# Feed-forward blocks that project the gained residual, with the root factor applied on eviction, and first pieces made across the layer's end

## What is computed

```python
def rmsnorm(x, g):
    xf = x.astype(F32)
    y = xf * lax.rsqrt(jnp.mean(xf * xf, axis=-1, keepdims=True) + NORM_EPS)
    return (y * g.astype(F32)).astype(x.dtype)

def swiglu_ffn(h, w_gate, w_up, w_down):
    return (jax.nn.silu(h @ w_gate) * (h @ w_up)) @ w_down

    for l in range(DEPTH):
        h = rmsnorm(x, P['ffn1_norm'][l])
        x = x + 0.5 * swiglu_ffn(h, P['ffn1_w_gate'][l], P['ffn1_w_up'][l], P['ffn1_w_down'][l])
        h = rmsnorm(x, P['mix_norm'][l])
...
        x = x + jnp.concatenate([y_a, y_b, y_c], axis=-1) @ P['w_out'][l]
        h = rmsnorm(x, P['xattn_norm'][l])
...
        x = x + cross_attend(h, mk, mv, P['xattn_w_q'][l], P['xattn_w_o'][l])
        h = rmsnorm(x, P['ffn2_norm'][l])
        x = x + 0.5 * swiglu_ffn(h, P['ffn2_w_gate'][l], P['ffn2_w_up'][l], P['ffn2_w_down'][l])
    y = rmsnorm(x, P['final_norm'])
```

## Time and profile before

| | |
|---|---|
| median of 3 runs | 1805.14 us (1805.0 to 1806.65) |
| the profiled execution | 1805.17 us |
| its span | 1803.4 us |
| PE busy, share of the span | 1638.5 us, 91% |
| DVE, ACT, POOL busy | 57%, 40%, 19% |
| mean granted PE clock | 0.939 of full |

### The profile page before, as it was taken

One profiled execution on the slowest core, in us unless ns is written; L12 is line 12 of the kernel. 1 busy time (PEld: TensorE's weight loads), 2 busy tenths in 40 slices (PEclk: granted clock), 3 DMA queues, 4 the chain that ended last, 5 costly groups with the idle time before them and its releaser, 6 DMA issues.

```text
span 1803.4 us, 31820 instructions
## 1 busy us (share of the span) xinstructions
PE 1638.5 (91%) x13650; PEld 1536.5 (85%) x13650; DVE 1021.6 (57%) x1469; ACT 712.4 (40%) x1212; POOL 342.0 (19%) x365
## 2 busy tenths in 40 slices
PE   7999989897789988999989999998877998799997
PEld 6999979774679768999989998897646896799996
DVE  5555459958453336554365544698584642555543
ACT  5443345322444334443344433452234442444432
POOL 0000019993010010000000000399910000100000
PEclk9999989896899989999989999898869999899998
DMA  6666634104255763444345576340043558444440
GB/s 229 260 243 250 265 122 141 66 2 107 106 187 209 278 269 131 164 164 164 140 163 205 215 280 234 113 140 30 2 142 117 188 206 337 182 162 166 164 164 27
DMA packets 39244, 303.63 MB, mean 168 GB/s; under 512 B 4736, under 2 KB 4896, under 8 KB 6304
## 3 DMA queue, kind: packets, MB, share of 16 engines
q1 hardware_dynamic: 36624, 287.67, 43.6%
q0 software_dynamic: 2192, 12.35, 2.5%
q10 hardware_dynamic: 288, 1.57, 0.2%
HBM read 291.82 MB, written 36.83 MB: 182 GB/s over the span
## 4 chain that ended last, share of the span: by engine, by line
PE 66%; POOL 17%; DVE 9%; ACT 4%; DMA 3%; issue 1%; SPq 0%; POOLq 0%; DVEq 0%; ACTq 0%
PE bank L578 20%; PE bank L579 20%; PE bank L580 20%; POOL arena L474 12%; POOL arena L490 5%; DMA slots<-stream 3%; DVE w_lo L1610 2%; ACT w_hi L1218 2%; DVE h_mem L1625 1%; DVE rs L1620 1%; DVE h_lo L1610 1%; PE bank L589 1%; PE bank L1134 1%; PE bank L1170 1%; PE bank L1119 1%
## 5 line engine op out<-in xcount | busy, mean ns | idle before, releaser
L1610 DVE TENSOR_TENSOR w_lo<-slots,w_hi 128x1024 fp32r<-128x1024 f32 x392 | 481.9, 1232 | 430.1 <-ACT w_hi L1218 429.4
L578 PE MATMUL bank<-h_hi,w_hi 128*128 128x288 f32 x2048 | 620.1, 303 | 45.8 <-DVE h_lo L1610 30.2
L579 PE MATMUL bank<-h_lo,w_hi 128*128 128x288 f32 x2048 | 611.5, 299 | 0.0
L580 PE MATMUL bank<-h_hi,w_lo 128*128 128x288 f32 x2048 | 609.0, 297 | 0.0
L1218 ACT CAST w_hi<-slots 128x1024 fp32r<-128x1024 f32 x392 | 410.1, 1048 | 388.6 <-PE bank L580 346.6
L578 PEld LDWEIGHTS bank<-h_hi,w_hi 128*128 128x128 f32 x2048 | 389.8, 190 | 56.4 <-DVE h_lo L1610 37.4
L580 PEld LDWEIGHTS bank<-h_hi,w_lo 128*128 128x128 f32 x2048 | 392.8, 192 | 0.0
L579 PEld LDWEIGHTS bank<-h_lo,w_hi 128*128 128x128 f32 x2048 | 391.9, 191 | 0.2
L474 POOL TENSOR_SCALAR arena<-arena,par_all 128x256 f32<-128x256 f32 x240 | 210.4, 899 | 5.5
L579 PE MATMUL bank<-hid_lo,w_hi 128*128 128x288 f32 x704 | 208.2, 296 | 0.0
L578 PE MATMUL bank<-hid_hi,w_hi 128*128 128x288 f32 x704 | 208.1, 296 | 0.0
(11 more groups left out here) (279 smaller groups left out, 1934.9 us busy)
## 6 DMA issues: line engine op xcount, KB each, us to landing
slots<-stream SPq DMA_DIRECT2D x244, 1024.0 KB, 5.0
out_win3k<-win3k SPq DMA_DIRECT2D x2, 4080.0 KB
out_win3v<-win3v SPq DMA_DIRECT2D x2, 4080.0 KB
out_win2k<-win2k SPq DMA_DIRECT2D x2, 2032.0 KB
out_win2v<-win2v SPq DMA_DIRECT2D x2, 2032.0 KB
con<-consts SPq DMA_DIRECT2D x1, 2276.0 KB, 10.8
arena<-mem_in POOLq DMA_DIRECT2D x2, 1024.0 KB, 5.2
out_memk<-arena POOLq DMA_DIRECT2D x2, 1024.0 KB, 7.4
```

What stands on the lines that cost most here:

```text
L578: mm(out, lhs[0], rhs[0], start=start, stop=False)
L579: mm(out, lhs[0], rhs[1], start=False, stop=False)
L580: return mm(out, lhs[1], rhs[0], start=False, stop=stop)
L1610: D(tt(out, src, hi.bitcast(F32), ALU.subtract), name)
```

## The change

1. **Feed-forward blocks** no longer normalise. ACT makes `h_hi` as x times the norm's weight in one activation with a per-partition scale (`gained_hi`), DVE makes `h_lo` as x times the weight minus `h_hi` (`gained_lo`), and PE projects that. The factor `rs` (one over the root, per token) comes in afterwards: the gate's eviction is now two DVE products (`gs` is gate times rs, `gs2` is gs times rs), tanh reads `gs`, and gate times up takes `gs2` and the raw up bank.
2. **PE** runs `sum_squares` after the first gate unit instead of before it. Tile 0 uses banks 4 and 5, tile 1 banks 6 and 3.
3. **In front of ffn2** the gained pieces are made piece by piece inside the output projection: `gained_hi` then the square after each `x_o` on ACT, `gained_lo` of the piece before between the split and the addition on DVE.
4. **Across the layer's end** `next_layer` makes pieces 0 to 3 of the next layer's `h_hi`, `h_lo` and squares, and its first two weight units, before the second half of the down projection ends. POOL adds the four squares (`presum(l, "next", EARLY)`). Buffers of units run on across layers (`w_slot`). A prologue does the same before layer 0.
5. **Additions into x** after the down projection are signalled one by one, `("ffn2", "x", k)`, not per half.
6. In the last layer `next_layer` makes the four squares for the final norm, with tiny writes to `idle` in the place of the weight units.

The core of the diff (`KT` is 8). The constants and PE:

```diff
+EARLY = KT // 2
+PRESUM = {"ffn1": EARLY, "mix": EARLY, "xattn": KT - 1, "ffn2": KT - 1}
+        def ffn_banks(t):
+            return ((4, 5), (6, 3))[t] if t < 2 else ((t % 2) * 2, (t % 2) * 2 + 1)
...
                 def ffn(tag):
-                    sum_squares(tag)
                     for t in range(FT):
-                        gb, ub = (t % 2) * 2, (t % 2) * 2 + 1
+                        gb, ub = ffn_banks(t)
                         claim(gb, (VL, (tag, "gated", t)))
                         claim(ub, (VL, (tag, "hid", t)))
...
+                            if t == 0 and o == 0:
+                                sum_squares(tag)
...
-                                claim(b, (VL, (tag, "x", half)))
+                                claim(b, (VL, (tag, "x", 4 * half + d)))
```

On ACT, the two new functions:

```diff
+            def gained_hi(l, tag, k, name):
+                g = PAR[tag] + k
+                SL.done(fn(h_hi[:, k, :], x[:, k, :], ACT.Copy, scale=par_all[:, l, g:g + 1]), (name, "hi", k))
+            def next_layer(l):
+                at = min(l + 1, DEPTH - 1)
+                for k in range(EARLY):
+                    if l >= 0:
+                        act.wait_ge(vector_done, VL.value(l, ("ffn2", "x", k)))
+                    gained_hi(at, "ffn1", k, "next")
+                    SL.done(fn(sq[:, k, :], x[:, k, :], ACT.Square), ("next", "sq", k))
+                for u in range(EARLY_UNITS):
...
+                    copy(w_hi[:, w_slot(l + 1, u), :], raw_unit(u), ("next", "hi_w", u))
```

On ACT, between the cross attention and ffn2:

```diff
-                def ready2(k):
+                for k in range(KT):
                     if k:
                         split(next_unit(UNITS["o"] + k - 1))
                     act.wait_ge(vector_done, VL.value(l, ("x_o", k)))
...
+                    gained_hi(l, "ffn2", k, "ffn2")
+                    square("ffn2", x, T, k)
```

On DVE, in a tile of the feed-forward block:

```diff
+                        dve.wait_ge(tensor_done, TL.value(l, (tag, "gate", t)))
+                        D(tt(gs[:, t % 2, :], bank[gb][:, 0:T], rs[:], ALU.mult), (tag, "gated", t))
+                        settle()
+                        D(tt(gs2, gs[:, t % 2, :], rs[:], ALU.mult))
+                        if t > 1:
+                            split(next_unit(first + 2 * t))
+                        settle()
                         dve.wait_ge(scalar_done, SL.value(l, (tag, "tanh", t)))
-                        D(stt(th2[:, t % 2, :], th[:, t % 2, :], 1.0, bank[(t % 2) * 2][:, 0:T], ALU.add, ALU.mult),
+                        D(stt(th2[:, t % 2, :], th[:, t % 2, :], 1.0, gs2, ALU.add, ALU.mult))
```

On DVE, in the output projection of the cross attention:

```diff
                     if t:
                         split(next_unit(UNITS["o"] + t - 1))
+                        gained_lo(l, "ffn2", t - 1, "ffn2", l)
                     dve.wait_ge(tensor_done, TL.value(l, ("o", "cols", t)))
                     b = (5, 6, 7, 0, 1, 2, 3)[t % 7]
                     D(tt(x[:, t, :], bank[b][:, 0:T], x[:, t, :], ALU.add), ("x_o", t))
```

More of the change, by code:

```diff
@@ L190, in done @@
             self.last = ins
-        if name is not None:
+        if name is not None and self.recording:
             assert self.at.setdefault(name, self.n) == self.n, name
@@ L279, in program @@
         th2 = take(2, T)
+        gs = take(2, T)
+        gs2 = take(T)
         top[0] = KT * T
@@ L441, in store, with presum @@
                 stores[name] = n_stores[0]
-            pool.sem_inc(pool_done, PL.total)
+            def presum(l, tag, n):
+                for k in range(1, n):
+                    pool.wait_ge(scalar_done, SL.value(l, (tag, "sq", k)))
+                    if k > 1:
+                        pool.wait_ge(pool_done, PL.value(l, (tag, "added", k - 1)))
+                    PL.done(nc.gpsimd.tensor_tensor(sq[:, 0, :], sq[:, 0, :], sq[:, k, :], ALU.add), (tag, "added", k))
+            pool.sem_inc(pool_done, PL.tail)
+            PL.begin_prologue()
+            presum(-1, "next", EARLY)
             pool.wait_ge(con_landed, 32)
@@ L513, in _ @@
                 store(memv_out[l], vx, "memv")
-                presum("ffn2")
+                presum(l, "ffn2", PRESUM["ffn2"])
+                PL.begin_tail()
+                presum(l, "next", EARLY)
             assert n_stores[0] == NSTORE
@@ L532, in next_unit, with w_slot, next_or_own @@
             return u + NW if all(not u < end <= u + NW for end in RUN_ENDS) else None
+        def w_slot(l, u):
+            return (l * NUNIT + u) % NW
+        def next_or_own(l, tag, k):
+            return (l - 1, "next") if tag == "ffn1" and k < EARLY else (l, tag)
+        def ffn_banks(t):
+            return ((4, 5), (6, 3))[t] if t < 2 else ((t % 2) * 2, (t % 2) * 2 + 1)
         def unit_head(u):
@@ L1202, in _ @@
             l = DEPTH - 1
-            for k in range(KT):
-                pe.wait_ge(scalar_done, SL.value(l, ("final", "sq", k)))
+            pe.wait_ge(pool_done, PL.value(l, ("next", "added", EARLY - 1)))
+            for k in (0, *range(EARLY, KT)):
+                if k:
+                    pe.wait_ge(scalar_done, SL.value(l, ("final", "sq", k)))
                 i = mm(bank[7][:, 0:T], ones, sq[:, k, :], start=k == 0, stop=k == KT - 1)
@@ L1593, in _, with gained_lo, next_layer @@
             cp = nc.vector.tensor_copy
+            def gained_lo(l, tag, k, name, by):
+                g = PAR[tag] + k
+                dve.wait_ge(scalar_done, SL.value(by, (name, "hi", k)))
+                VL.done(stt(h_lo[:, k, :], x[:, k, :], par_all[:, l, g:g + 1], h_hi[:, k, :].bitcast(F32), ALU.mult, ALU.subtract),
+                        (name, "h_lo", k))
+            def next_layer(l):
+                at = min(l + 1, DEPTH - 1)
+                for k in range(EARLY):
+                    gained_lo(at, "ffn1", k, "next", l)
+                for u in range(EARLY_UNITS):
+                    if l == DEPTH - 1:
+                        VL.done(nc.vector.memset(idle[:, 2 + u:3 + u], 0.0), ("next", "lo", u))
+                        continue
+                    dve.wait_ge(scalar_done, SL.value(l, ("next", "hi_w", u)))
+                    w = w_slot(l + 1, u)
+                    VL.done(tt(w_lo[:, w, :], raw_unit(u), w_hi[:, w, :].bitcast(F32), ALU.subtract), ("next", "lo", u))
+            VL.begin_prologue()
+            next_layer(-1)
+            for k in range(EARLY, KT):
+                VL.done(nc.vector.memset(idle[:, k:k + 1], 0.0))
             for l in range(DEPTH):
@@ L1647, in ffn @@
                             split(next_unit(u))
-                        dve.wait_ge(tensor_done, TL.value(l, (tag, "down", half)))
+                        if half and tag == "ffn2":
+                            VL.begin_tail()
+                            next_layer(l)
                         for d in range(4):
                             k = 4 * half + d
+                            if d == 0:
+                                dve.wait_ge(tensor_done, TL.value(l, (tag, "down", half)))
                             D(stt(x[:, k, :], bank[4 + d if half == 0 else d][:, 0:T], 0.25, x[:, k, :], ALU.mult, ALU.add),
-                              (tag, "x", half) if d == 3 else None)
-                for u in range(NW):
-                    split(u)
+                              (tag, "x", k))
+                for k in range(EARLY, KT):
+                    gained_lo(l, "ffn1", k, "ffn1", l)
+                split(EARLY_UNITS)
                 ffn("ffn1")
@@ L2065, in _ @@
                     D(tt(x[:, t, :], bank[b][:, 0:T], x[:, t, :], ALU.add), ("x_o", t))
+                gained_lo(l, "ffn2", KT - 1, "ffn2", l)
                 split(next_unit(UNITS["o"] + KT - 1))
```

129 lines of the change are left out of this document (79 added, 50 removed).

## The result

The changed kernel takes 1782.31 us (median of four runs, 1780.0 to 1788.71) beside 1805.16 us before; the ratio is 0.988 with a 95% interval of 0.9865 to 0.9893. Run again later beside the kernel before, it took 1784.6 us against 1805.8, ratio 0.989 (0.9873 to 0.9907). The eight runs together have a median of 1784.0 us and a spread of 9.4 us. The kernel before stays within 1.65 us in the first series, but spreads by up to 8.9 us in the series of the experiments (1803.88 to 1812.77), so a difference of 2 or 3 us between two medians says little by itself. The predicted time was 1782.0, the range 1774 to 1791. The profiled execution took 1783.72 us, 21.45 less than that of before.

What follows compares the result with a forecast made beforehand. PE, busy 91% of the span, was taken as the bound, its idle time as the gain; 3.0 + 1.6 + 1.1 + 12.5 + 2.9 + 1.1 + 1.05 = 23.2 us off 1805.17 gave 1782.0 us, range 1774 to 1791.

Steps and rivals of the forecast that it cites:

- start: Kernel start, before layer 0: 3.0 us won; bounds 1.5 (slow clock throughout) and 4.5 (full clock).
- norm after ffn1: Norm behind the first feed-forward block: root 1.6 us earlier in layer 0, 2.9 in layer 1, 1.1 there at 1.2 GHz.
- ffn2's start: From output projection into second feed-forward block: 1.1 us won per layer; bounds 0.6 lost to 2.5 won, 7.5 with loop free.
- layer's end: From down projection into next layer's second weight unit: 12.5 us won, with a 0.6 us stall for piece 4, then full clock.
- last norm: Final norm: root 3.4 us after the first addition instead of 4.45, a gain of 1.05 us.
- attention stages: Stages between the feed-forward blocks: they move as a block, their waits for DMA stay, no gain.
- the loop doesn't bind: Rival at ffn2's start: PE's wait is one addition long, 6.4 us more won per layer, 1769; chance 0.11 (1765 to 1773).
- claim and loop: At ffn2's start: PE claims bank 5 before its first gate matmul; the DVE and ACT turn in `o` grows to 3.94 us.
- The table load: ACT's load takes 1.28 us, root right behind it, against the skill's 2.66; at the kernel's start it begins at 6.8.
- The tiles: 88 feed-forward tiles: two more DVE operations of 0.45 us each cost zero, with 0.4 us of cover per tile.
- the slower rival: DVE can't hold the feed-forward tile: at 0.35 us over, 88 tiles cost 30.8 us, 1813; chance 0.04.
- Restarts paid twice: Rival in the feed-forward blocks: units follow too late after the reciprocal, each block gives back 3 us, 1794; chance 0.10.

Runs made afterwards that it cites:

- The experiment that opens the loop: Changed kernel, but in `o` DVE adds each tile before making the next weight unit's rest and the previous tile's `h_lo`: 1770.73 us.
- both edits: Changed kernel with tile 0 on banks 4 and 6, tile 1 on 5 and 3, and DVE's addition in `o` ahead of rest and piece: 1767.57 us.

## Why the prediction was right, step by step

The total was right, and most of its steps too, but that it met the first median within 0.3 us is luck. The eight runs have 1784.0, and in the two profiles the steps add up to 1.7 and 2.9 us less than the forecast. The table sets them beside the two profiled executions of the kernel after (us won against the profiled execution of before).

| step | predicted | first | second |
|---|---|---|---|
| start | 3.0 | 2.05 | 3.01 |
| norm after ffn1, layer 0 (to the root) | 1.6 | 1.56 | 0.09 |
| ffn2's start, layer 0 | 1.1 | 1.16 | 1.29 |
| layer's end | 12.5 | 12.78 | 12.79 |
| norm after ffn1, layer 1 | 2.9 | 1.42 | 1.50 |
| ffn2's start, layer 1 | 1.1 | 1.40 | 1.35 |
| last norm | 1.05 | 1.0 | 1.0 |
| attention stages, both layers | 0 | +0.96 | +0.17 |
| four blocks, unit 1 to first addition | 0 | -0.85 | -0.85 |
| sum | 23.2 | 21.5 | 20.3 |

- **ffn2's start.** Size and mechanism were right: additions every 3.90 us (I said 3.94), a wait of 5.13, the second unit gained 1.16 us. Two small misses cancel in it: the clock stayed at 0.50 for 5.2 us, not 4.2, so the unit took 5.6 us and not 5.1, while PE started 0.3 us earlier than forecast and the two products took 0.75 us and not 1.0. I had refused the 7.5 us that one would expect at first sight. The experiment that opens the loop gives 7.4 and 7.2 us in the two layers. My rival "the loop doesn't bind" priced this at 6.4. Of the two reasons that I named, claim and loop, the loop is the stronger one, 13.3 us against 5.9.
- **The layer's end.** 12.78 against 12.5. The stall is 0.47, not 0.6, and full clock after it was the right choice. With the early pieces late this stage gives back 9.1 us, the largest single part of what the change wins. The 16.5 us by which that kernel is slower overstate it, since 5.9 of them are the edit's own cost at the last norm.
- **The norm after ffn1** is the mis-sized term. "At 3.4 after it the gain is 2.9" took full clock for PE's four products, and the root did come 3.44 us after the first addition in layer 0 of the first profile. Where the clock is slow it is 4.9, as in layer 1 of that profile and in both layers of the second. I had the low bound of 1.1 for layer 1, and had written that layer 0 would then gain nothing. Both happened. The low bound was the likelier value. The thirteen profiles of kernels with this order hold 26 such norms. The reciprocal came 3.86 or 3.87 us after the first addition in 5 of them and 4.3 to 5.4 us in the others.
- **The start.** The table load began at 6.76 and PE's first matmul at 13.68, where I had put them at 6.8 and 13.5. In the first execution nearly all matmuls of unit 0 start 0.24 us apart, the step that the earlier trace rows have at 0.50, and the gain of 2.05 lies between my slow bound of 1.5 and the 3.0. (The profile's clock row gives 1.00 for 13.60 to 19.60; here I go by the steps.) The second came to 20.95, the predicted time.
- **The attention stages**, put at nothing, are a sum that hides its parts. Layer 0 lost 0.8 us and layer 1 won 1.8 in the first profile, 1.9 and 2.0 in the second, for code that the change hardly touches. That they nearly cancel is luck, and no run here explains them.
- **The tiles** cost nothing, and PE has no wait inside the blocks. The cover was 0.75 us at the place where I counted 0.4, so the slower rival was farther off than I said.
- **The blocks** lose 0.21 us each in this way of counting, without a wait in them. Unit 1's first matmul is recorded 0.2 us early behind the products of the sum: it starts at 897.32, its fourth at 897.92, where the steps of three are 0.40 us elsewhere. So the four rows of the table that end at unit 1 show 0.2 us too much each, and the row of the blocks gives it back.
- **Restarts paid twice** didn't happen. The rest of unit 3 was ready at 687.07, and PE came to it at 689.79, 2.7 us later, within my 2 to 3 us.
- **The table load.** In the first profile the load starts at 234.32, and the root follows 1.40 us after that:

```profile
234.32 1.28 ACT L1298 ACT_TABLE_LOAD   x1
...
235.72 0.39 ACT L1300 ACTIVATE rs<-bank 128x288 f32<-128x288 f32 x1
```

The Trainium skill (ScalarE: Activation LUTs, What ACT_TABLE_LOAD costs) has about 2.66 us for each switch, load and drain together. By that the root could not come before 236.98, so the trace decides against it, as the earlier trace rows did.

## What to carry to other kernels

Where two engines hand one item to and fro in program order, add up the whole turn before adding a step to it: 0.73 us more in each of seven turns that had no room put PE out of work for 5 us and cost it the clock behind that. The cure was not less work but the short operation that frees the other engine, ahead of the long ones. Whether more work on an engine costs anything is asked place by place: the same 0.98 us were free before a wait that another engine ends, and 13 us dearer at the end of the tile.

## What the runs showed of the hardware

- PE's clock after a pause isn't settled by the length of the pause alone. The waits of 5.1 us at ffn2's start were followed by 1.2 GHz, a wait of 0.6 us by 2.4 GHz. But 2.81 us at the same place of the same program were followed by 1.00 in one execution and by a mean of 0.64 in another, and 1.50 and 0.83 us close together by 0.50. This accounts for part of the 9.4 us between runs of the kernel after.
- DVE's piece of `h_lo`, which reads two tiles in SBUF, takes 1.07 us instead of 0.51 while POOL adds two SBUF tiles of 128x288, and 0.51 again once POOL's additions are gone. The Trainium skill (SBUF — State Buffer, Who interferes with whom) has DVE and GpSimd share a pair of ports under an exclusive lock. The traces agree that the two engines get in each other's way here. That the piece waits for the whole of POOL's addition they don't show: with both edits it starts 0.06 us after an addition of 0.82 us and is longer by 0.56, where the rest of the addition is 0.76.
